# First block of a two-block model: gates between projection tiles, square roots and index scores at other tiles, four Gelu buffers

## The reference, cut to what matters

```python
u = modulate(h, norm1_g, sh1, sc1)
xr, gr, q, ckv, qi, ki, wi, mg = split(u @ w_in)
x = causal_dwconv(xr, conv_w, conv_b)                       # width 1280, 4 taps
r = sigmoid(blocks(x) @ w_a + b_a); i = sigmoid(blocks(x) @ w_x + b_x)
log_a = -8 * softplus(-lam) * r
hr = scan(exp(log_a), sqrt(-expm1(2 * log_a)) * (i * x))    # a linear recurrence over the sequence
y_a = (gelu(gr) * hr) @ w_rnn_out
score = (wi * relu(qi @ ki)).sum(heads)                     # the best 128 keys of each query, by top_k
att = attention(q, rmsnorm(ckv), selected keys)
ga, gb = split(sigmoid(mg))
h = h + g1 * ((ga * y_a + gb * (att @ w_att_out)) @ w_out)
h = h + g2 * hier_moe(modulate(h, norm2_g, sh2, sc2))       # 32 experts, two for each position
```

## Time and profile before

| | us |
|---|---|
| median of 3 runs | 3142.61 |
| lowest and highest | 3139.91, 3147.86 |
| the profiled execution | 3141.53 |
| its span, first to last instruction | 3139.7 |
| TensorE busy in the span | 3028.9 |
| VectorE, ScalarE, GpSimd busy | 1611.3, 1001.1, 975.3 |
| mean granted clock of TensorE | 0.989 |

### The profile page before, as it was taken

One profiled execution on the slowest core, in us unless ns is written; L12 is line 12 of the kernel. 1 busy time (PEld: TensorE's weight loads), 2 busy tenths in 40 slices (PEclk: granted clock), 3 DMA queues, 4 the chain that ended last, 5 costly groups with the idle time before them and its releaser, 6 DMA issues.

```text
span 3139.7 us, 35184 instructions
## 1 busy us (share of the span) xinstructions
PE 3028.9 (96%) x13964; PEld 2103.2 (67%) x13964; DVE 1611.3 (51%) x2790; ACT 1001.1 (32%) x1527; POOL 975.3 (31%) x423
## 2 busy tenths in 40 slices
PE   7999999999999989999999999999999999999998
PEld 4777756743333356776757788887676766778886
DVE  5698956455555445475566522221737466632223
ACT  3653233300000044324353322123423445332212
POOL 3243103210000044433213544446432321544433
PEclk8999999999999999999999999999999999999999
DMA  6236312599999922121211222222121120222221
GB/s 256 94 113 242 116 47 92 198 364 427 427 427 427 425 109 83 68 81 54 81 54 67 81 94 94 94 96 103 65 81 67 58 104 14 94 81 94 94 95 53
DMA packets 64819, 448.47 MB, mean 143 GB/s; under 512 B 8526, under 2 KB 8814, under 8 KB 12448
## 3 DMA queue, kind: packets, MB, share of 16 engines
q1 hardware_dynamic: 60336, 436.25, 36.2%
q0 software_dynamic: 3760, 8.11, 0.7%
q10 hardware_dynamic: 576, 2.10, 0.2%
HBM read 445.93 MB, written 4.21 MB: 143 GB/s over the span
## 4 chain that ended last, share of the span: by engine, by line
PE 82%; DVE 8%; DMA 7%; ACT 2%; issue 1%; SPq 0%; DVEq 0%; ACTq 0%
PE ps L461 16%; PE ps L463 16%; PE ps L462 16%; DMA mring<-w 6%; PE ps L2551 4%; PE ps L804 3%; PE ps L783 2%; PE ps L2615 2%; PE ps L784 2%; PE ps L785 2%; PE ps L2463 2%; PE ps L450 2%; DVE P L832 2%; PE ps L817 1%; PE ps L906 1%
## 5 line engine op out<-in xcount | busy, mean ns | idle before, releaser
L520 POOL TENSOR_TENSOR w_lo<-wring,w_hi 128x2048 fp32r<-128x2048 f32 (+1 forms) x284 | 854.3, 3025 | 1606.3 <-ACT w_hi L510 1606.3
L461 PE MATMUL ps<-x_hi,w_hi 128*128 128x512 f32 (+1 forms) x1480 | 582.0, 393 | 8.8 <-ACT lru_t L1704 4.5
L463 PE MATMUL ps<-x_hi,w_lo 128*128 128x512 f32 (+1 forms) x1480 | 577.2, 390 | 0.0
L510 ACT ACTIVATE w_hi<-wring 128x2048 fp32r<-128x2048 f32 x176 | 335.9, 1911 | 306.7 <-PE ps L461 235.0
L462 PE MATMUL ps<-xf_lo,w_hi 128*128 128x512 f32 x1080 | 421.5, 390 | 0.0
L461 PEld LDWEIGHTS ps<-x_hi,w_hi 128*128 128x128 f32 (+1 forms) x1480 | 278.1, 188 | 77.7 <-ACT gb L1728 5.2
L463 PEld LDWEIGHTS ps<-x_hi,w_lo 128*128 128x128 f32 (+1 forms) x1480 | 278.1, 188 | 59.1
L2551 PE MATMUL ps<-mring,xT__96 128*64 128x512 f32 x512 | 238.5, 602 | 12.7 <-DMA mring<-w 7.2
L2552 PE MATMUL ps<-mring,xT__96 128*64 128x512 f32 x512 | 238.6, 602 | 0.0
L462 PEld LDWEIGHTS ps<-xf_lo,w_hi 128*128 128x128 f32 x1080 | 203.4, 188 | 41.5
L1432 DVE TENSOR_TENSOR g_f<-ps,g_f 128x512 f32<-128x512 f32 x44 | 30.4, 692 | 363.8 <-PE ps L463 350.4
(11 more groups left out here) (554 smaller groups left out, 5408.7 us busy)
## 6 DMA issues: line engine op xcount, KB each, us to landing
mring<-w SPq DMA_DIRECT2D x192, 1024.0 KB, 23.4
wring<-wlayers SPq DMA_DIRECT2D x148, 1024.0 KB, 4.7
wring<-wfirst SPq DMA_DIRECT2D x44, 1024.0 KB, 4.8
mods<-wrest SPq DMA_DIRECT2D x16, 1024.0 KB, 4.7
wmodS<-wmod SPq DMA_DIRECT2D x3, 2048.0 KB, 17.9
rp<-rpb POOLq DMA_DIRECT2D x16, 192.0 KB, 2.8
hT<-xT SPq DMA_DIRECT2D x1, 2048.0 KB, 9.1
wmodS<-wmod SPq DMA_DIRECT2D x2, 1024.0 KB, 26.4
```

Source lines behind the costliest of these rows:

```text
L461: said(pe.matmul(bank, wh[:, 0:m], hi[:, k, :], start=(k == 0), stop=False))
L463: ins = pe.matmul(bank, wl[:, 0:m], hi[:, k, :], start=False, stop=(k == nk - 1))
L510: act.activation(w_hi[:, q % HI_SLOTS, :], wring[:, home(g), :], ACT.Copy).then_inc(hi_rdy, 1)
L520: ins = pool.tensor_tensor(w_lo[:, home(slot), o:o + n], wring[:, home(slot), o:o + n], w_hi[:, q % HI_SLOTS, o:o + n].bitcast(F32), ALU.s ...
```

## The change

The first two xr tiles are multiplied together, chunk by chunk, with their weights packed to match. The gate weights leave the stream and come in one transfer of 1.25 MB into `rgw`, where the index queries lie later; the stream is two slots shorter, and `home` is shifted so that the later places stay. The pair of gate products of chunk n follows xr tile n + 2, the last two pairs follow the two ckv tiles; ScalarE's and VectorE's lists follow that order, with the same operations. Exponentials and roots 0 and 1 now stand ahead of the first qi read-out, roots 2 and 3 behind the fourth qi and the wi read-out, and the other six between Gelus. Gelus go to four buffers (`gelu_out`). The mg sigmoids wait for one recurrence at a time, as their output lies over the decays. Index scores, their Relu and the norm of ckv come two mg tiles later (`IX_LAG`), the last two pairs of scores behind the first two q tiles, and ScalarE's wait for the modulation behind the first of these. In the routing of the experts two semaphores become one. The diff, without the lines that only rename or repeat:

```diff
@@ constants, stream_plan, build
+IX_LAG = 2
 def home(slot):
-    return (slot + 1) % SLOTS
+    return (slot + 3) % SLOTS
-    first = [("xr", RC * DC), ("rg", 2 * RC), ("ckv", KVC * DC), ("qi", 4 * DC), ("ki", DC),
+    first = [("xr", RC * DC), ("ckv", KVC * DC), ("qi", 4 * DC), ("ki", DC),
-    unsplit = [("rg", "ckv"), ("uk", "att_out")]
+    unsplit = [("uk", "att_out")]
+        rgw = at("rgw", 169, [P, 2 * RC * P])
+        def gelu_out(n):
+            return lru_t[:, n % 2, 2 if n % 4 < 2 else 0, :]
@@ def _(sp):
             for s in range(1, n_slots1):
+                if s == 2:
+                    sp.dma_start(rgw[:], wrg).then_inc(rg_in, 16)
@@ def _(act):
-            for n in range(RC):
+            def conv_in(n):
                 weights_hi(act, one["xr"] + n * DC)
-                if n == RC - 1:
-                    act.activation(lru_t[:, 0, 2, 0:1], ones[:, 0:1], ACT.Sigmoid)
                 b = A.take(act)
...
-            def decay(n):
...
-            for n in range(RC):
+            def gates_in(n):
                 if n >= 2:
                     act.wait_ge(gated_x, n - 1)
                 act.activation(lru_t[:, n % 2, 0, :], A.take(act), ACT.Sigmoid, bias=V("b_rg_a")[:, n:n + 1]).then_inc(A.free, 1)
                 act.activation(lru_t[:, n % 2, 1, :], A.take(act), ACT.Tanh, scale=0.5, bias=hbx[:, n:n + 1]).then_inc(A.free, 1)
-                weights_hi(act, one["rg"] + 2 * n)
-                if n >= 1:
-                    decay(n - 1)
+            def decay(n):
...
+            conv_in(0)
+            conv_in(1)
+            act.activation(lru_t[:, 0, 2, 0:1], ones[:, 0:1], ACT.Sigmoid)
+            for n in range(2, RC):
+                conv_in(n)
+                gates_in(n - 2)
+                if n >= 3:
+                    decay(n - 3)
+            for m in range(KVC):
+                weights_hi(act, one["ckv"] + m * DC)
+                act.activation(ckv[:, m, :], A.take(act), ACT.Copy).then_inc(A.free, 1)
+                gates_in(RC - KVC + m)
+                decay(RC - KVC + m - 1)
             decay(RC - 1)
...
             def gelu(n):
                 weights_hi(act, one["gr"] + n * DC)
-                if n >= 2:
-                    act.wait_ge(gh_rdy, n - 1)
-                act.activation(lru_t[:, n % 2, 2, :], A.take(act), ACT.Gelu_apprx_tanh).then_inc(A.free, 1)
-            parts = [(ckv[:, c, :], P, 1.0) for c in range(KVC)] + [(qi[:, m, :], P, 1.0) for m in range(4)]
+                if n >= 4:
+                    act.wait_ge(gh_rdy, n - 3)
+                act.activation(gelu_out(n), A.take(act), ACT.Gelu_apprx_tanh).then_inc(A.free, 1)
+            for n in range(2):
+                square_root(n)
+            parts = [(qi[:, m, :], P, 1.0) for m in range(4)]
             parts += [(ki[:], P, 1.0), (wi_rows[0:IDX_HEADS, :], IDX_HEADS, IDX_SCALE)]
-            roots = {0: (0,), 1: (1,), 2: (2,), 3: (3,), 5: (4,), 6: (5,), 7: (6,)}
+            roots, roots_gelu = {3: 2, 5: 3}, {0: 4, 2: 5, 3: 6, 5: 7, 7: 8, 8: 9}
             for n, (to, rows, scale) in enumerate(parts):
                 act.activation(to, A.take(act)[0:rows, :], ACT.Copy, scale=scale).then_inc(A.free, 1)
...
+                weights_hi(act, one["qi"] + n * DC)
+                if n in roots:
+                    square_root(roots[n])
             for n in range(RC):
                 gelu(n)
-                if n in (1, 3, 4):
-                    square_root(7 + (1, 3, 4).index(n))
+                if n in roots_gelu:
+                    square_root(roots_gelu[n])
...
-            act.wait_ge(gh_rdy, RC)
...
             for m in range(2 * DC):
                 weights_hi(act, one[f"mg{m // 2}"] + (m % 2) * DC)
                 to = mixT if m < DC else gb
+                if m < DC:
+                    act.wait_ge(h_rdy, m + 1)
+                elif m == DC:
+                    act.wait_ge(gh_rdy, RC)
                 act.activation(to[:, m % DC, :], A.take(act), ACT.Sigmoid).then_inc(A.free, 1)
...
+                index_relu(m - IX_LAG)
-                if m == 0:
+                if m == IX_LAG:
                     root(act)
-            act.wait_ge(mod_used, 1 + MOD_SLOTS)
             for h in range(HEADS):
                 weights_hi(act, one["q"] + h * DC)
+                if h < IX_LAG:
+                    index_relu(2 * DC - IX_LAG + h)
+                if h == 0:
+                    act.wait_ge(mod_used, 1 + MOD_SLOTS)
                 act.activation(qT[:, h, :], A.take(act), ACT.Copy).then_inc(A.free, 1)
@@ def _(dve):
+            for n in range(RC):
+                convolve(n)
+                if n >= 2:
+                    gated_input(n - 2)
+            for n in range(RC - 2, RC):
+                gated_input(n)
...
-            behind = {5: (0,), 6: (1, 2), 7: (3, 4), 8: (5, 6), 9: (7, 8, 9)}
+            behind = {4: (0,), 5: (1, 2), 6: (3,), 7: (4, 5), 8: (6, 7), 9: (8, 9)}
@@ def _(pe):
-            for n in range(RC):
-                tile3(pe, A.claim(pe), one["xr"] + n * DC, *u, DC, wait=(lambda k: pe.wait_ge(u_rdy, k + 1)) if n == 0 else None).then_inc(A.full, 1)
-            for n in range(RC):
+            first = A.claim(pe), A.claim(pe)
+            for k in range(DC):
+                pe.wait_ge(u_rdy, k + 1)
+                for n, b in enumerate(first):
+                    wh, wl = chunk(pe, one["xr"] + 2 * k + n)
+                    said(pe.matmul(b, wh, u[0][:, k, :], start=(k == 0), stop=False))
+                    pe.matmul(b, wh, u[1][:, k, :], start=False, stop=False)
+                    ins = pe.matmul(b, wl, u[0][:, k, :], start=False, stop=(k == DC - 1))
...
+            def gate_products(n):
                 pe.wait_ge(conv_rdy, n + 1)
                 for g in range(2):
                     b = A.claim(pe)
-                    w = chunk(pe, one["rg"] + 2 * n + g)
+                    w = rgw[:, (2 * n + g) * P:(2 * n + g + 1) * P]
...
+            pe.wait_ge(rg_in, 16)
+            for n in range(2, RC):
+                tile3(pe, A.claim(pe), one["xr"] + n * DC, *u, DC).then_inc(A.full, 1)
+                gate_products(n - 2)
             for m in range(KVC):
                 tile3(pe, A.claim(pe), one["ckv"] + m * DC, *u, DC).then_inc(A.full, 1)
+                gate_products(RC - KVC + m)
...
             for m in range(2 * DC):
                 tile3(pe, A.claim(pe), one[f"mg{m // 2}"] + (m % 2) * DC, *u, DC).then_inc(A.full, 1)
+                if m == IX_LAG:
+                    squares_pe(pe, KVC)
+                if m == IX_LAG + 1:
+                    spread_pe(pe)
+                index_scores(m - IX_LAG)
             for m in range(HEADS):
                 tile3(pe, A.claim(pe), one["q"] + m * DC, *u, DC).then_inc(A.full, 1)
+                if m < IX_LAG:
+                    index_scores(2 * DC - IX_LAG + m)
@@ the host's packing
-    parts["rg"] = np.stack([i["w_rg_a"][0], i["w_rg_x"][0]], 1).reshape(-1, P, P)
+    parts["xr"][:2 * DC] = parts["xr"][:2 * DC].reshape(2, DC, P, P).transpose(1, 0, 2, 3).reshape(-1, P, P)
+        "wrg": np.ascontiguousarray(np.stack([i["w_rg_a"][0], i["w_rg_x"][0]], 1).reshape(-1, P, P).transpose(1, 0, 2).reshape(P, -1)),
```

More of the change, by code:

```diff
@@ L2395, in _ @@
             u = x_hi, x_lo[1]
[L2396 to L2398 removed]
+            first = A.claim(pe), A.claim(pe)
[6 more added lines that the diff above has]
+                    ins = pe.matmul(b, wl, u[0][:, k, :], start=False, stop=(k == DC - 1))
+                    if k == DC - 1:
+                        ins.then_inc(A.full, 1)
+            def gate_products(n):
                 pe.wait_ge(conv_rdy, n + 1)
@@ L2424, in _, with index_scores @@
             ins.then_inc(A.full, 1)
-            for m in range(2 * DC):
-                tile3(pe, A.claim(pe), one[f"mg{m // 2}"] + (m % 2) * DC, *u, DC).then_inc(A.full, 1)
-                if m == 0:
-                    squares_pe(pe, KVC)
-                if m == 1:
-                    spread_pe(pe)
-                for k in range(2 * m, 2 * m + 2):
+            def index_scores(j):
+                for k in range(2 * j, 2 * j + 2) if j >= 0 else ():
                     qb, h = divmod(k, IDX_HEADS)
@@ L2437, in _ @@
                               ki[r:r + 64, 0:(qb + 1) * P], start=True, stop=True).then_inc(ix_score, 1)
+            for m in range(2 * DC):
+                tile3(pe, A.claim(pe), one[f"mg{m // 2}"] + (m % 2) * DC, *u, DC).then_inc(A.full, 1)
+                if m == IX_LAG:
[3 more added lines that the diff above has]
+                index_scores(m - IX_LAG)
             for m in range(HEADS):
                 tile3(pe, A.claim(pe), one["q"] + m * DC, *u, DC).then_inc(A.full, 1)
+                if m < IX_LAG:
+                    index_scores(2 * DC - IX_LAG + m)
             pe.wait_ge(ckv_rdy, KVC)
```

44 lines of the change are left out of this document (20 added, 24 removed).

## The result

| kernel | median | runs | fastest to slowest | profiled execution | its span |
|---|---|---|---|---|---|
| before | 3140.86 us | 15 | 3136.75 to 3147.86 | 3141.53 us | 3139.7 us |
| after | 3151.59 us | 15 | 3142.39 to 3153.77 | 3150.40 us | 3148.6 us |

The ratio after to before is 1.0033, with a 95% interval of 1.0026 to 1.0039: **about 10 us slower**. The prediction was 3140.1 us, 2.5 us less than before. The sign is wrong, the time lies outside the range, and one term was missing. The prediction also held that less than 0.3% can't be told from nothing; this interval is 0.13% wide.

The account below looks back on a forecast made before the run. TensorE was taken as the bound (82% of the span). First tiles and gates -0.1, new wait +3.0, Gelu wait and clock -5.8, last Gelu +0.4 gave -2.5 us: 3142.61 to 3140.1 us; range 3132 to 3149.

Parts of the forecast that it names:

- Two first tiles: First xr tiles: third tile starts at 52.7, not 53.26, after TensorE waits 2.1 us for GpSimd's low half; 0.6 us won.
- Gates between tiles: Xr and ckv tiles: gate pairs wait for the read-out two tiles back, taking 0.5 us more; this work ends at 131.7.
- New wait of 3.0 us near 143: First index tiles: TensorE waits 3.0 us for ScalarE's exponentials, two roots and first copy, with no clock fall.
- Gelu wait and its clock: Gelu tiles near 180 us: the 4.2 us wait and 1.6 us of half clock behind it go, 5.8 us won.
- Last Gelu at 223.6: End of the Gelu tiles: last bank free at 223.6, mixer gate tile 0 at 223.7; 0.4 us later.
- The dearer table switches: Roots between Gelus: the skill page's price of about 2.66 us per switch would put mg tile 0 at 229; set aside.
- VectorE's chain with 1.8 us to spare: Recurrences to sums of squares: chain starts at 142.8, sums end at 238.3; TensorE asks behind third mg tile, at 240.1.
- The third rival: VectorE's chain becomes the bound through late roots, TensorE waiting behind the third mg tile; +6.3 us, 3148.9; chance 0.15.
- Attention at 400.2, search just hidden: Attention starts at 400.2 for 402.73; VectorE's search ends 8.4 us later, at 400.5, needed at 400.8.

Follow-up runs that it names:

- x1: The kernel after with GpSimd's low-half passes of nine weight blocks cut into four pieces; 3138.5 us, ratio to before 0.9993.
- x6: The kernel after with the edits of x1, x3 and x4 together; 3137.3 us, ratio to before 0.9993.
- x9: x6 with the last square root moved behind the last Gelu; 3134.6 us, ratio to before 0.9979.
- x4: The kernel after with square roots 0 and 1 behind the read-outs of the first two index tiles, not ahead of them; 3147.5 us, ratio to before 1.0022.
- x12: The kernel before with four Gelu buffers and roots 6 to 9 moved behind Gelu outputs 0, 2, 4 and 6; 3141.5 us, ratio to before 1.0001.
- x7: The kernel before with four Gelu buffers in place of two and no other edit; 3140.0 us, ratio to before 1.0001.
- x10: x9 without the pieces, so with whole low-half passes; 3136.9 us, ratio to before 0.9995.
- x2: The kernel before with the same weight blocks' low-half passes cut into four pieces; 3140.7 us, ratio to before 0.9997.
- x8: The kernel after with the same low-half passes cut into two pieces, not four; 3151.1 us, ratio to before 1.0032.
- x3: The kernel after with the sums of squares and first index scores one mixer gate tile later; 3143.9 us, ratio to before 1.0017.

## Why the prediction was wrong, point by point

- **Two first tiles, -0.6.** Right: the third tile at 52.67, 52.84 with the 0.17, for 52.7, waiting for GpSimd's low half. The wait was 1.04, not 2.1, since the two tiles ended later; the start is nearly the same.
- **Gates between tiles, +0.5; first index tile at 131.7.** Right: eight waits of 0.47 (3.7 in all), the first index tile at 130.80 + 0.17 = 130.97, 0.7 better than said. Neither part was undone in a run of its own; this rests on the trace, and on x1, x6 and x9, which keep both parts and are not slower than the kernel before.
- **New wait of 3.0 us near 143.** Right in place and size: 2.68 at 144.66. The clock did fall behind it in the kernel after (0.79 from 142 to 150), which I priced at 1.6 us and didn't take. x4: this wait and what follows from it are worth 3.5 us.
- **Gelu wait and its clock, -5.8.** The wait near 180 went, and x12 shows 6.0 us won at the mixer gates. But the reason given was wrong in part (a root ahead of the first Gelu, not the two buffers, x7), and the step took it as won for good. x12 shows that it isn't.
- **Last Gelu at 223.6, +0.4.** Wrong: the first mixer gate tile came at 228.28, behind a wait of 4.50. The step followed ScalarE's queue through roots and table loads and never asked when the fifth product, for which Gelu 8 waits, is there. ScalarE waited 3.96 us for it. The dearer table switches that the prediction weighed and set aside would have put this tile at 229, near what came, but by luck: the loads of the kernel after take 1.28 us, as before, and this wait makes the difference.
- **The step that failed: VectorE's chain with 1.8 us to spare.** It took the chain's length from the kernel before, 94.6 us from the first recurrence to the last product, and moved it as a block. Its start was right (141.99 for 142.8). Its length was 245.29 + 5.27 - 141.99 = 108.6, 14.0 more. Of these the products are 12.5 (21.6 - 9.1), the late roots 2.96 (0.28 + 2.46 + 0.22 of VectorE's waiting), less the 1.73 of waiting that before had the earlier trace rows. A duration that includes a collision was carried over to a place where the collision is another. What could have told it: GpSimd runs one pass per weight block through this whole stretch, 23.0 us of 50.5, and a product of 0.67 alone appeared in pairs of 1.95 to 2.37 in the kernel before.
- **The third rival had the place and the late chain**, the wait behind the third mixer gate tile, and a price of +6.3. Its cause, the roots, was wrong: by the rows they were 3 us late and not 9, and x1 takes the loss away without touching one. Its chance, 0.15, was too low, since 1.8 us to spare against a stage of 95 us is no margin.
- **Attention at 400.2, search just hidden.** The search ended at 409.64 + 0.90 = 410.5 and VectorE stood idle 4.89 us ahead of the attention: not the bound, as said. ScalarE's wait for the modulation, which I let fall into the second q tile's time, did so here; in x10, with TensorE earlier, it didn't.

With the products' term set right the sum fits: x1, the same change with short products, measures -2.2 us, where the sum said -2.5. Its interval, -4.7 to +0.6, would fit other sums as well; at the attention x1 is 1.2 us early, with the clock fall of 1.7 us near 144 that the sum left out.

Open: whether the other VectorE instructions with two SBUF operands, the modulation products of 1.2 us that take up to 5.6 within passes, cost anything at the end. TensorE waits for them in none of these traces but in x10 (2.56 us), and no run took that away.

## What to carry to other kernels

A busy time from a profile belongs to the offset at which it was taken: where two engines lock each other out, an edit that moves one against the other changes the length of instructions that the diff doesn't touch, so list what runs beside each instruction of a chain before moving the chain. A wait of the main engine is worth its length only up to the next place where it meets the chain it waited for (x12: 6.0 us won, all given back from some 9 us later on), so look for that place first. And a long GpSimd pass beside a chain of short VectorE instructions is cheap to cut into quarters: x1 gained 12.6 us, and where no chain was bound (x2) it cost nothing that could be measured, though four quarters take 5.05 us for the 4.6 of a whole pass.

## What the runs showed of the hardware

- A product of two SBUF operands waits until a GpSimd pass that is already running has ended: 0.67 us alone, up to 4.74 behind a pass of 4.6 us. Between two pieces of a pass that follow each other at once one held product got in, and the next piece waited for it (1.74 us for 1.29 in x1), so halves gave nothing to pairs (x8, 5.17 us) and quarters more than half (x1, 2.94).

- The same wait doesn't always cost the clock. After the wait of 2.68 us for the first index copy the granted clock from 142 to 150 us was 0.79 in the kernel after, in x1 and in x8, and 1.00 in x3; the program is the same in all four up to there. A clock fall behind a wait of this length is a matter of chance, here worth 1.7 us (8 x 0.21), and not a term to be set at zero. The window of the kernel after, then of x3:

```profile
142.00:150.00 8.00, 5.34 (x16) 4.24 (x17) 7.66 (x11) 4.87 (x7) 3.51 (x1) 0.79 0.40 131
...
142.00:150.00 8.00, 5.99 (x26) 4.97 (x27) 7.66 (x12) 4.41 (x7) 4.17 (x1) 1.00 0.41 131
```
